# Layer 1 attention: GpSimd multiplies the probabilities by the inverse of their sum, and the outputs are no longer scaled by a spread made on TensorE

## The reference, cut to what matters

```python
def _band_attend(q, k, v, q_pos, k_pos, rel_table):
    bias = ...                                   # learned, by clipped relative position
    logits = jnp.einsum('bthd,bshd->bhts', q, k) * (DH ** -0.5) + bias[None]
    logits = jnp.where((k_pos >= 0)[None, None, None, :], logits, -jnp.inf)
    p = jax.nn.softmax(logits, axis=-1)
    return jnp.einsum('bhts,bshd->bthd', p.astype(v.dtype), v)
```

## Time and profile before

| | us |
|---|---|
| median of 3 runs | 3065.2 (3063.87 to 3065.74) |
| profiled execution: span of its instructions | 3063.2 |
| layer 1 attention, 64 units: first to last score | about 1980 to 2195 |
| layer 1 attention, end of the sample side | about 2228 |

### The profile page before, as it was taken

The page is one execution under the profiler, slowest core; times in us unless marked ns, Lnnn a source line. Parts: engine busy times, 40 slices in busy tenths (PEclk is TensorE's granted clock), DMA queues, the critical chain, the costliest instruction groups (busy, mean ns, idle before and its releaser), DMA issues. The chain is left out here.

```text
span 3063.2 us, 60271 instructions
## 1 busy us (share of the span) xinstructions
PE 2910.1 (95%) x25097; PEld 2707.8 (88%) x25097; DVE 1613.1 (53%) x2967; ACT 958.8 (31%) x2005; POOL 1292.9 (42%) x1053
## 2 busy tenths in 40 slices
PE   6999999996789999999999999999899999999998
PEld 5859999765689999999999999866689999999998
DVE  6399999655646644434346400056537644444445
ACT  3341111355433433332101311266525333332001
POOL 2111223382533877776334232100124877775334
PEclk9999999998899999999999999999999999999999
DMA  5816763533241122224221232253121222214222
GB/s 214 252 67 215 239 206 134 166 127 112 100 171 51 58 83 77 84 84 138 87 84 63 80 103 100 74 196 103 50 86 49 70 77 84 84 68 156 79 75 73
DMA packets 160464, 338.82 MB, mean 111 GB/s; under 512 B 21032, under 2 KB 94528, under 8 KB 152192
## 3 DMA queue, kind: packets, MB, share of 16 engines
q1 hardware_dynamic: 120720, 281.74, 27.3%
q10 hardware_dynamic: 39472, 53.21, 4.9%
HBM read 268.30 MB, written 79.49 MB: 114 GB/s over the span
## 5 line engine op out<-in xcount | busy, mean ns | idle before, releaser
L109 PE MATMUL tr_acc<-tr_quad_hi,ah_ring_hi 128*128 128x264 f32 x2432 | 694.5, 286 | 8.3 <-DVE tr_kept L1188 2.2
L111 PE MATMUL tr_acc<-tr_quad_hi,ah_ring_lo 128*128 128x264 f32 x2432 | 692.6, 285 | 0.0
L110 PE MATMUL tr_acc<-tr_quad_lo,ah_ring_hi 128*128 128x264 f32 x2432 | 690.2, 284 | 0.0
L575 POOL TENSOR_TENSOR ah_ring_lo<-ah_raw,ah_ring_hi 128x512 fp32r<-128x512 f32 (+1 forms) x402 | 555.0, 1386 | 159.5 <-ACT ah_ring_hi L918 146.5
L109 PEld LDWEIGHTS tr_acc<-tr_quad_hi,ah_ring_hi 128*128 128x128 f32 x2432 | 458.5, 189 | 10.6 <-DVE tr_kept L1188 2.6
L110 PEld LDWEIGHTS tr_acc<-tr_quad_lo,ah_ring_hi 128*128 128x128 f32 x2432 | 458.7, 189 | 0.1
L111 PEld LDWEIGHTS tr_acc<-tr_quad_hi,ah_ring_lo 128*128 128x128 f32 x2432 | 458.2, 188 | 0.0
L573 POOL CAST ah_ring_hi<-ah_raw 128x512 fp32r<-128x512 f32 (+1 forms) x162 | 102.2, 631 | 591.3 <-PE tr_acc L111 525.3
L109 PE MATMUL tr_acc<-tr_part_hi,ah_ring_hi 128*128 128x352 f32 x1038 | 335.5, 323 | 2.0 <-DVE tr_kept L1226 2.0
L110 PE MATMUL tr_acc<-tr_part_lo,ah_ring_hi 128*128 128x352 f32 x1038 | 332.8, 321 | 0.0
L111 PE MATMUL tr_acc<-tr_part_hi,ah_ring_lo 128*128 128x352 f32 x1038 | 332.5, 320 | 0.0
(11 more groups left out here) (397 smaller groups left out, 6421.3 us busy)
## 6 DMA issues: line engine op xcount, KB each, us to landing
f_ada_w<-in_w_ada_dram SPq DMA_DIRECT2D x48, 1024.0 KB, 5.5
scratch_inner<-tr_kept ACTq DMA_DIRECT2D x88, 264.0 KB, 2.3
tr_staged<-scratch_inner SPq DMA_DIRECT2D x44, 528.0 KB, 4.2
ah_raw<-in_w_gate_dram SPq DMA_DIRECT2D x44, 512.0 KB, 3.6
ah_raw<-in_w_up_dram SPq DMA_DIRECT2D x44, 512.0 KB, 4.5
ah_raw<-in_w_down_dram SPq DMA_DIRECT2D x64, 256.0 KB, 3.3
f_raw<-in_w_dram SPq DMA_DIRECT2D x24, 512.0 KB, 8.0
out_z_dram<-f_stage ACTq DMA_DIRECT2D x60, 176.0 KB, 1.9
```

Source lines behind the costliest of these rows:

```text
L109: pe.matmul(out, w_hi, hi, start=start, stop=False)
L110: pe.matmul(out, w_hi, lo, start=False, stop=False)
L111: return pe.matmul(out, w_lo, hi, start=False, stop=stop)
L575: pool.tensor_tensor(lo[:, 0:width], own, hi[:, 0:width].bitcast(F32), ALU.subtract).then_inc(w_ready, 1)
```

## The change

It has four parts, all in `attention_phase`, all for the call without a mask.

1. The spread goes: `spread_inverse` on PE, `copy_spread` on ACT and the `spread` tiles. `finish` becomes a copy of `out` into `oT`. The numbering of the turns, which also fixes which engine copies which group, has no entry for the spread any more; within a unit the alternation by s-2+j stays.
2. `weigh(u)` comes: two GpSimd instructions for each unit that multiply the probabilities of a head in place by `inv` (a scalar per partition). `turns(u)` waits for `weighed` in place of `prob_ready`.
3. `inverse` stands one step earlier on DVE: `inverse(s-1)` in step s, at the same place within the step.
4. GpSimd's list is put in a new order. The corners of pairs 0 and 1 come first, then the units; the corners of pair g+1 come behind `weigh` of block 3 of pair g, and one weight split of the next phase behind `weigh` of block 5 of pairs 0 to 5.

```diff
+            def mask_band(g):
+                b = g % 2
+                if g:
+                    pool.wait_ge(bias_in[b], 16 * ((g + 1) // 2))
+                pool.memset(bias[b][0:CHUNK, :, width - CHUNK:width], MASKED).then_inc(band_masked, 1)
+                pool.memset(bias[b][CHUNK:P, :, 0:CHUNK], MASKED).then_inc(band_masked, 1)
+                pool.wait_ge(band_masked, 2 * g + 2)
+
+            def weigh(u):
+                n = keys[units[u][1]]
+                pool.wait_ge(inv_ready, u + 1)
                 for hd in range(2):
...
+                    own = prob[2 * (u % 3) + hd][:, 0:n]
+                    pool.tensor_scalar(own, own, inv[:, 2 * u + hd:2 * u + hd + 1], 1.0, ALU.mult, ALU.mult).then_inc(weighed, 1)
+
+            if mask is None:
+                mask_band(0)
+                mask_band(1)
+                for u, (g, i) in enumerate(units):
+                    weigh(u)
+                    if i == 3 and 1 <= g < pairs - 1:
+                        pool.wait_ge(weighed, 2 * u + 2)
+                        mask_band(g + 1)
+                    if ahead and i == 5 and g < AHEAD:
+                        ahead.split(pool, g)
...
             if ahead:
-                pool.wait_ge(band_masked, 2 * pairs)
-                for i in range(AHEAD):
-                    ahead.split(pool, i)
                 ahead.done(pool)
...
-                pe.wait_ge(prob_ready, 2 * u + (1 if cols.stop <= keys[i] else 2))
+                pe.wait_ge(prob_ready if mask is not None else weighed, 2 * u + (1 if cols.stop <= keys[i] else 2))
...
-                    if (s - 3) % 4 == 3:
+                    if mask is not None and (s - 3) % 4 == 3:
                         spread_inverse((s - 3) // 4)
...
                 dve.wait_ge(out_done, 4 * quad + 4)
-                dve.wait_ge(act_copied, act_no[spread_no[quad] + 1])
                 if part == 0 and g >= 2:
                     dve.wait_ge(stored[b], 16 * (g // 2))
+                if mask is None:
+                    dve.tensor_copy(oT[b][:, 512 * part:512 * part + 512], out[quad % 2][:]).then_inc(finished, 1)
+                    return
...
-                if 0 <= s - 2 < U:
-                    inverse(s - 2)
+                done = s - (2 if mask is not None else 1)
+                if 0 <= done < U:
+                    inverse(done)
...
-                if s >= 3 and (s - 3) % 4 == 3:
+                if mask is not None and s >= 3 and (s - 3) % 4 == 3:
                     copy_spread((s - 3) // 4)
```

More of the change, by code:

```diff
@@ L2159, in attention_phase @@
         for j in range(4):
-            if j == 2 and s >= 3 and (s - 3) % 4 == 3:
+            if mask is not None and j == 2 and s >= 3 and (s - 3) % 4 == 3:
                 spread_no[(s - 3) // 4] = len(by_act)
@@ L2192, in attention_phase @@
         prob = [prob_all[:, max(keys) * a:max(keys) * a + max(keys)] for a in range(6)]
-        spread = [sb(f"{name}_spread{b}", [P, 4 * P]) for b in range(2)]
+        spread = [sb(f"{name}_spread{b}", [P, 4 * P]) for b in range(2)] if mask is not None else None
         probT = [sb(f"{name}_probT{a}", [P, 2 * max(keys)]) for a in range(2)]
@@ L2226, in attention_phase @@
         prob_ready, turned, act_copied, dve_copied = (m.sem(f"{name}_{x}") for x in ("prob", "turned", "act_copied", "dve_copied"))
-        inv_ready, out_done, finished = (m.sem(f"{name}_{x}") for x in ("inv", "out", "finished"))
+        inv_ready, out_done, finished, weighed = (m.sem(f"{name}_{x}") for x in ("inv", "out", "finished", "weighed"))
         block = m.block()
@@ L2327, in side_masks @@
                     pool.tensor_tensor(s_bias[g][:], s_bias[g][:], s_mask[:], ALU.add).then_inc(s_masked, 1)
-            for u, (g, i) in enumerate(units):
+            def mask_band(g):
                 b = g % 2
-                if i == 0 and g:
+                if g:
                     pool.wait_ge(bias_in[b], 16 * ((g + 1) // 2))
[L2333 to L2339, removed]
-                for hd in range(2):
[L2341 to L2346, removed]
+                pool.memset(bias[b][0:CHUNK, :, width - CHUNK:width], MASKED).then_inc(band_masked, 1)
+                pool.memset(bias[b][CHUNK:P, :, 0:CHUNK], MASKED).then_inc(band_masked, 1)
+                pool.wait_ge(band_masked, 2 * g + 2)
@@ new lines, in weigh @@
+            def weigh(u):
+                n = keys[units[u][1]]
+                pool.wait_ge(inv_ready, u + 1)
+                for hd in range(2):
+                    own = prob[2 * (u % 3) + hd][:, 0:n]
[10 more added lines that the diff above has]
+                        ahead.split(pool, g)
+            else:
+                for u, (g, i) in enumerate(units):
+                    b = g % 2
+                    if i == 0 and g:
+                        pool.wait_ge(bias_in[b], 16 * ((g + 1) // 2))
+                    for hd in range(2):
+                        if u >= 2:
+                            pool.wait_ge(logits, 2 * (u - 2) + hd + 1)
+                        pool.tensor_tensor(extra[2 * (u % 2) + hd][:, 0:keys[i]], bias[b][:, hd, width - keys[i]:width],
+                                           mask[:, score_offset(i):score_offset(i + 1)], ALU.add).then_inc(extra_ready, 1)
+                    if u == U // 2:
+                        side_masks()
@@ L2526, in finish @@
                 dve.wait_ge(out_done, 4 * quad + 4)
-                dve.wait_ge(act_copied, act_no[spread_no[quad] + 1])
                 if part == 0 and g >= 2:
                     dve.wait_ge(stored[b], 16 * (g // 2))
+                if mask is None:
+                    dve.tensor_copy(oT[b][:, 512 * part:512 * part + 512], out[quad % 2][:]).then_inc(finished, 1)
+                    return
+                dve.wait_ge(act_copied, act_no[spread_no[quad] + 1])
                 dve.tensor_tensor(oT[b][:, 512 * part:512 * part + 512], out[quad % 2][:], spread[quad % 2][:], ALU.mult
```

## The result

The kernel after takes 3071.98 us (median of 14 runs, 3069.07 to 3075.61) against 3064.64 for the kernel before (14 runs beside it, 3062.51 to 3067.91): ratio 1.0023, 95% interval 1.0016 to 1.0031, or 7 us slower. The forecast was 3072.6. The profiled execution took 3070.77 with a span of 3068.0, 4.8 above the span before.

A forecast was written before the change was run, and what follows sets the result against it. PE, busy for 95% of the span, was taken as the bound, waiting for DVE in steps 3 to 5. 19.2 us late - 12.05 gained + 0.3 tight place = 7.4 slower: 3072.6 us, range 3066 to 3085.

The forecast's parts named there:

- The gain: Spreads removed in steps 2 and 6 of the pairs and behind the last unit: 0.87, 0.68 and 1.2 us, 12.7 in all.
- The last spread: Spread behind the last unit, ahead of the sample side: its removal gains 1.2 us, carried to the phase's end.
- The weighing: GpSimd's weigh in steady pairs: 0.72 us for 640 columns, 0.50 for 384, 0.29 for 128; cost 0.3 us in all.
- the mark that I had set as a sign of being wrong: Signs against the forecast: TENSOR_SCALAR above 0.8 us, with turns waiting for weighed and a pair of 27 us or more.
- The first hold: Corners of pair 1 wait for their bias ahead of weigh(0): the turns of unit 0 start 8.0 us late.
- The second hold: First split, ahead of weigh(6), waits for the first two weight loads: the turns of unit 6 start 17.1 us late.
- Slow clock: After the idle stretch before unit 6, PE resumes at half speed for 4 to 5.7 us: 2.1 us lost.
- The later splits, corners and the wait of VectorE for the second exponential: Later GpSimd waits and the earlier inverse's wait on DVE, in steady pairs: covered, costing nothing.
- the tight place: Step 4 of a pair, block 2: weighing takes 1.19 of 1.26 us, 0.07 to spare; cost 0.05 us a pair, 0.3 in all.
- One hold only: Rival: weights land before GpSimd asks, so only the bias wait counts; 3.9 us faster, 3061.3 us; chance 0.10.
- Neither hold: Rival: what stands ahead of weigh is passed, so both waits vanish; 12.7 - 0.3 us faster, 3052.8 us; chance 0.06.
- The slow weighing: Rival: weigh runs at two-input price (1.56 us for 640 columns), adding 23 us; 30.4 slower, 3095.6 us; chance 0.11.

The follow-up runs named there:

- e5_noscale: The kernel before without the spread and with no weigh, so outputs are not divided by their sums: 3052.44 us, ratio 0.9956.
- e6_twice: e8_third with a second GpSimd instruction of the same shape (times 1.0) behind each weighing of a head: 3086.27 us, ratio 1.0069 to the kernel before.
- e1_corners: The kernel after with the corners of pair 1 moved behind the weighing of block 3 of pair 0: 3071.95 us, ratio 1.0021 to the kernel before.
- e2_splits: The kernel after with the six weight splits behind block 5 of pairs 2 to 7 instead of 0 to 5: 3063.13 us, ratio 0.9990.
- e4_loads: The kernel after with the four weight loads issued ahead of the sample side's keys and values: 3062.20 us, ratio 0.9989 to the kernel before.
- e3_both: The kernel after with the edits of e1_corners and e2_splits together: 3059.66 us, ratio 0.9976 to the kernel before.
- e8_third: e3_both with the corners of pair 2 behind block 5 of pair 1 instead of block 3: 3052.06 us, ratio 0.9961 to the kernel before.
- e7_inverse: e8_third with the inverse back in step s for unit s-2: 3279.08 us in one run, 227 above e8_third.

## Why the prediction was right, step by step

- The gain. Steps 2 and 6 gave 0.87 and 0.68 us, pair by pair, the forecast's figures; e5_noscale shows the whole at 12.8 us by the medians and 12.3 by the units' time, forecast 12.7. The last spread gave 0.9 and not 1.2: VectorE's first logit of the sample side came 1.34 us behind its scores, not 1.1.
- The weighing. I took 0.72 us for 640 columns; it is 0.80. The slope was right (0.83 ns a column between 128 and 640), the instruction with a scalar from SBUF has 0.08 us more than one with a constant (0.80 and 0.72 in e6_twice), which no row of before could show. The two weighings of 384 columns took 1.15 and not 1.05, so the room of 0.07 in step 4 became a lack of 0.03: 0.03 us a pair, forecast 0.05. The 802 ns lie on the mark that I had set as a sign of being wrong (above 0.8 us), and yet a pair took 26.28 us, far from the 27 that went with it: a unit's two widest weighings need 1.6 us and had 2.0 or more, so the mark was badly placed.
- The first hold. 8.0 us was forecast. The turns of unit 0 came 11.0 us into the phase instead of 3.4: 7.5. That it counts for nothing in the sum is what e1_corners shows.
- The second hold. 17.1 forecast, 16.3 measured. The first weights were there 36.8 us into the phase; I had put them at 37.7, from the third load's landing and the DMA rate. Slow clock 2.1 forecast, 1.7 measured.
- The later splits, corners and the wait of VectorE for the second exponential: nothing, as forecast; pairs 2 to 6 are alike within 0.02 us whether they hold a split or not.
- The sum. 19.2 - 12.05 + 0.3 = 7.4 forecast. The trace has 18.0 - 10.6 - 0.9 = 6.5 up to the sample side; the medians of 14 runs have 7.3, in an interval of 5 to 9.5. The misses don't cancel: the second hold, its slow clock and the tight place came out 0.8, 0.4 and 0.1 us less slow than forecast, and only the last spread, which gained 0.3 less, goes the other way; the sum of the terms was 0.9 too high. So the mechanism and each size are right to under 1 us, and that forecast and medians agree to 0.1 is luck. Over the experiments the units' time and the medians differ from the kernel before by nearly the same: 6.0 and 6.0 in e1_corners, -3.9 and -2.8 in e2_splits, -4.0 and -3.7 in e4_loads, -6.8 and -6.3 in e3_both, -12.0 and -13.1 in e8_third. So hardly anything of the change lies behind the units. What of the last 1 us here is chance can't be told from single traces.
- The rivals. One hold only: e2_splits and e4_loads are this case; forecast 3.9 below the kernel before, measured 2.8 and 3.7 by the medians. Neither hold: forecast 3052.8 (12.4 below); e8_third is 3052.06. But the case was thought of as one with two waits, and there is a third, at the corners of pair 2. I had cleared it ("come at about 2037, their bias landed before 2026.5"), rightly for the kernel after and wrongly for a kernel with neither hold; e3_both found it. The slow weighing was under-priced at 23 us: in e6_twice the two instructions together take 1.52 us for 640 columns, against 1.56 at the two-input price, and cost 31 to 34; a part of the difference is the clock, which this price left out.

## What to carry to other kernels

When work that others wait for is put on an engine with a list in order, go through everything else on that list, above all waits for DMAs, and ask when each comes true and what now stands behind it: an idle engine's waits cost nothing only as long as nothing follows them. Holds that end at a landing don't add up; the latest takes in the others, and removing it may uncover one that it had pushed out of the way, so check every one again against the new times. Where waits of 1 us and more recurred, they cost their own length and stretches of half speed besides: a price made of the waits alone came out too low by a sixth in e6_twice and by almost half in e7_inverse. And a helper that is covered at 1.6 us a unit may have only hundredths to spare at its narrowest step: keep it one step ahead of its reader.

## What the runs showed of the hardware that I had not expected

- A GpSimd multiplication by a scalar per partition costs 375, 588 and 802 ns for 128, 384 and 640 columns; with a constant in its place 0.72 us for 640, 0.08 less.
- In e7_inverse PE waited 1.5 to 2.5 us in nearly every step, and the mean granted clock was 0.71 over 435 us, which is half speed for 58% of the time. The waits for GpSimd are 118 us and the phase grew by some 224, so such a wait cost about twice its own length. In e6_twice PE waited up to 1.2 us two or three times in a pair, and the clock fell to half in four stretches of a few us (mean 0.97 over 230 us). In e8_third, where the steps that wait do so for about 0.5 to 0.7 us, the clock stayed at full speed:

```profile
1985.00:2190.00 205.00, 190.64 (x1766) 129.56 (x1763) 129.40 (x392) 123.82 (x318) 96.12 (x151) 1.00 0.39 130
```
